# 32 of the 384 dense tokens take their down products from gathered rows; the gate product carries gate times activation; ScalarE builds three of eight one-hots

## The reference, cut to what matters

```python
q = (tokens @ w_query).reshape(Ntok, 8, 2, 128)
s = einsum('nhpd,hpkd->nhpk', q, sub_keys)          # 128 scores per head and half
s_top, i_top = top_k(s, 16)
cand = s_top[:, :, 0, :, None] + s_top[:, :, 1, None, :]   # 256 candidates
best, pos = top_k(cand, 16)                          # 16 experts per head: 128 per token
gate = softmax(best)
a = gelu(einsum('nd,nhkd->nhk', xb, expert_down[idx]))
out = einsum('nhk,nhkd->nd', gate * a, expert_up[idx])
```

## Time and profile before

| | |
|---|---|
| median of 3 runs | 1718.04 us |
| the profiled execution | 1719.09 us, its span 1717.4 us |
| PE busy | 1666.0 us, 97% |
| PEld (weight loads) busy | 1494.0 us, 87% |
| DVE busy | 1136.0 us, 66% |
| ACT busy | 672.5 us, 39% |
| POOL busy | 835.2 us, 49% |
| DMA | 423.38 MB, mean 247 GB/s |
| granted clock | 0.996 |

### The profile page before, as it was taken

How to read it: one execution, slowest core, us unless ns; L and a number is a source line. 1 busy time by engine, 2 the same in 40 slices (tenths; PEclk the granted TensorE clock), 3 DMA queues, 4 the chain that set the end, 5 groups by cost and what they waited for, 6 DMA issues and landing times.

```text
span 1717.4 us, 26045 instructions
## 1 busy us (share of the span) xinstructions
PE 1666.0 (97%) x8905; PEld 1494.0 (87%) x8905; DVE 1136.0 (66%) x2253; ACT 672.5 (39%) x972; POOL 835.2 (49%) x483
## 2 busy tenths in 40 slices
PE   7999999999999999999999999998999999999998
PEld 5788787868999999999999999997887878878886
DVE  4154552031295999796898888205878777878787
ACT  5342433342334343434444444333333333333333
POOL 3462374312255878786576666554333333434230
PEclk9999999999999999999999999999999999999999
DMA  4222243213635988887899999749999999999993
GB/s 172 89 96 74 74 148 123 86 50 101 207 133 189 297 285 276 285 286 255 312 322 324 332 339 348 263 146 335 321 355 335 352 330 352 339 348 351 342 347 146
DMA packets 148395, 423.38 MB, mean 247 GB/s; under 512 B 14320, under 2 KB 67568, under 8 KB 147440
## 3 DMA queue, kind: packets, MB, share of 16 engines
q1 hardware_dynamic: 93472, 237.53, 41.2%
q0 software_dynamic: 36864, 134.23, 21.8%
q10 hardware_dynamic: 18000, 50.89, 7.5%
HBM read 373.32 MB, written 49.28 MB: 246 GB/s over the span
## 4 chain that ended last, share of the span: by engine, by line
PE 58%; issue 20%; DMA 9%; POOL 9%; DVE 2%; ACT 1%; SPq 0%; POOLq 0%; ACTq 0%; DVEq 0%
PE psum L1136 18%; PE psum L1137 18%; PE psum L1138 18%; POOL w_low L367 9%; DMA arena<-down_rows,kept 4%; DMA arena<-hid_dram 4%; PE psum L1403 3%; DMA arena<-up_in 1%; DVE arena L1028 1%; PE psum L1389 1%; DMA kept<-down_in 1%; ACT w_high L459 0%; DVE arena L926 0%; DVE arena L1022 0%; DVE wgt_low L1067 0%
## 5 line engine op out<-in xcount | busy, mean ns | idle before, releaser
L367 POOL TENSOR_TENSOR w_low<-kept,w_high 128x1024 fp32r<-128x1024 f32 x212 | 517.4, 2443 | 481.2 <-ACT w_high L459 480.1
L1136 PE MATMUL psum<-hT_high,w_high 128*128 128x384 f32 (+1 forms) x1408 | 492.2, 350 | 7.3 <-POOL w_low L367 4.1
L1138 PE MATMUL psum<-hT_high,w_low 128*128 128x384 f32 (+1 forms) x1408 | 485.3, 345 | 0.0
L1137 PE MATMUL psum<-hT_low,w_high 128*128 128x384 f32 (+1 forms) x1408 | 485.1, 345 | 0.0
L1136 PE MATMUL psum<-up_high,wgt_high 128*128 128x512 f32 x768 | 301.2, 392 | 10.4 <-DVE wgt_low L1067 10.4
L1137 PE MATMUL psum<-up_low,wgt_high 128*128 128x512 f32 x768 | 299.8, 390 | 0.0
L1138 PE MATMUL psum<-up_high,wgt_low 128*128 128x512 f32 x768 | 299.7, 390 | 0.0
L459 ACT ACTIVATE w_high<-kept 128x1024 fp32r<-128x1024 f32 x212 | 224.1, 1058 | 192.5 <-DMA kept<-front_w 71.7
L1136 PEld LDWEIGHTS psum<-hT_high,w_high 128*128 128x128 f32 x1408 | 264.8, 188 | 19.2 <-issue 4.5
L1138 PEld LDWEIGHTS psum<-hT_high,w_low 128*128 128x128 f32 x1408 | 264.6, 188 | 10.3
L1137 PEld LDWEIGHTS psum<-hT_low,w_high 128*128 128x128 f32 x1408 | 264.9, 188 | 9.8 <-issue 0.5
(11 more groups left out here) (197 smaller groups left out, 1982.6 us busy)
## 6 DMA issues: line engine op xcount, KB each, us to landing
kept<-down_in SPq DMA_DIRECT2D x128, 512.0 KB
arena<-up_in SPq DMA_DIRECT2D x128, 512.0 KB
kept<-front_w SPq DMA_DIRECT2D x100, 512.0 KB
gate_dram<-arena ACTq DMA_DIRECT2D x6, 4096.0 KB, 15.9
arena<-gate_dram SPq DMA_DIRECT2D x32, 768.0 KB, 8.8
hid_dram<-arena ACTq DMA_DIRECT2D x112, 192.0 KB
arena<-hid_dram SPq DMA_DIRECT2D x112, 192.0 KB
kept<-x_in ACTq DMA_DIRECT2D x4, 512.0 KB, 5.0
```

The source lines that it names most:

```text
L367: nc.gpsimd.tensor_tensor(w_low[:, s, :], ring[:, s, :], w_hi[:, s, :].bitcast(F32), ALU.subtract).then_inc(low_ready, 1)
L1136: nc.tensor.matmul(out, lhs[0], rhs[0], start=first, stop=False)
L1137: nc.tensor.matmul(out, lhs[0], rhs[1], start=False, stop=False)
L1138: return nc.tensor.matmul(out, lhs[1], rhs[0], start=False, stop=last)
```

## The change

The last 32 tokens of dense tile 2 (the *edge*) leave the down product: `first_product`, Gelu, hid and its store have 352 columns (DE). Their 128 dot products are taken from gathered rows. 32 tokens × 128 slots are laid out as 128 partitions × 32 slots, so 32 more gathers and dots (`row_stream` mixes them with the 128 sparse ones: ROWS is 160); `edge_h` holds h of the 32 tokens four times over. ACT moves the edge's indices, and later its Gelu values back, by four small DMAs each. The edge's gates are multiplied by these Gelu values before they are transposed (`hk_last`), and the hid columns of the edge are ones in the up product, set by DVE's memsets in the buffers that it reads. For that, tile 2 is chosen first and transposed last, at step 24. AHEAD becomes 68, the steps carry 10 gathers in 6, the last 12 blocks up to two each.

In steps 0 to 43 DVE writes five of the eight second one-hots; ACT writes three (`hot_tails`) as relu(gate − gate·|iota − index|). 

```diff
 TILES_LAST = (ST, 0, 1, 2)
-EXP_AT = (16, 36, 56)
-TURN_AT = (20, 40, 60)
+CHOSEN = (DT - 1, 0, 1)
+EXP_AT = (16, 40, 64)
+TURN_AT = (24, 48, 68)
...
 RING_A, RING_B, RING_C = 5, 4, 8
-DOTS_SCORES = ((2, 2, 2, 2),) * 3
-DOTS_CAND = (1, 1, 1, 1)
-DOTS_HOT = (6, 6, 6)
-DOTS_A = 54
-DOTS_STEP = (2, 1, 2, 1, 2, 1)
-DOTS_B = GROUPS * sum(DOTS_STEP)
+EDGE = 32
+PARTS = P // EDGE
+EDGE_SLOTS = SLOTS // PARTS
+DE = DN - EDGE
+E0 = P - EDGE
+ROWS = SLOTS + EDGE_SLOTS
+DOTS_SCORES = (3, 2, 2, 2)
+DOTS_CAND = (1, 1, 1, 2)
+DOTS_HOT = 6
+DOTS_CHOICES = 60
+DOTS_A = 65
+DOTS_STEP = (2, 1, 2, 1, 2, 2)
+FIRST_EDGE = 32
+TAIL = 3
+TAIL_STEPS = DE // TB
+EDGE_GELU, EDGE_GATE, EDGE_TURN = 16, 19, 24
...
+def row_stream():
+    stream, own, edge = [], 0, 0
+    for k in range(ROWS):
+        if edge < EDGE_SLOTS and k >= FIRST_EDGE and (k % 2 == 0 or k >= DOTS_A):
+            stream.append((True, edge))
+            edge += 1
+        else:
+            stream.append((False, own))
+            own += 1
+    return stream
+STREAM = row_stream()
+EDGE_DONE = max(k for k in range(ROWS) if STREAM[k][0]) + 1
...
                     pool.wait_ge(dot_done, k - ahead + 1)
-                nc.gpsimd.indirect_dma_start(ring[slot], None, down_rows,
-                                             bass.IndirectOffsetOnAxis(idx3[:, k:k + 1].bitcast(U32), 0))\
+                edge, j = STREAM[k]
+                if edge and j == 0:
+                    pool.wait_ge(edge_moved, 2 * 16 * PARTS)
+                nc.gpsimd.indirect_dma_start(ring[slot], None, down_rows, bass.IndirectOffsetOnAxis(
+                    (edge_idx if edge else idx3)[:, j:j + 1].bitcast(U32), 0))\
...
-            pool.wait_ge(hk_ready, DT)
-            pool.wait_ge(hk_tr, DT)
+            pool.wait_ge(hk_ready, DT - 1)
+            pool.wait_ge(hk_tr, DT - 1)
...
                 for _ in range(DOTS_STEP[i % PER_GROUP] if i < DURING else 2):
-                    if k < SLOTS:
+                    if k < ROWS:
...
+            act.wait_ge(ffnn.h, DT)
+            for q in range(PARTS):
+                act.dma_start(edge_h[q * EDGE:(q + 1) * EDGE], hn[E0:P, DT - 1, :].rearrange("p (k n) -> p k n", k=KC))\
+                    .then_inc(edge_moved, 16)
...
                               r * 32 + 16 * (s // 2), r * 4 + (s + 3))
+            def turned_out(t, turned):
+                rows = turned.rearrange("p (a b) -> p a b", a=3)
+                step.put(nc.scalar.activation(tail_neg[:, t * P // TB:(t + 1) * P // TB, :],
+                                              rows[:, 2, :].rearrange("p (g e) -> p g e", e=TB)[:, :, TB - TAIL:TB],
+                                              ACT.Copy, scale=-1.0))
+                step.end()
+                nc.scalar.activation(hkT[:, :, t * P:(t + 1) * P], rows, ACT.Copy).then_inc(hkT_out, 1)
...
                 early_tiles(EXP_AT[n], TURN_AT[n])
-                act.wait_ge(hk_tr, n + 1)
-                nc.scalar.activation(hkT[:, :, n * P:(n + 1) * P], psum[:, 0, 0:3 * P].rearrange("p (a b) -> p a b", a=3), ACT.Copy)\
-                    .then_inc(hkT_out, 1)
+                if n == 0:
+                    act.wait_ge(idx_ready, 2)
+                    for q in range(PARTS):
+                        act.dma_start(edge_idx[q * EDGE:(q + 1) * EDGE, :],
+                                      idx_last[E0:P, q * EDGE_SLOTS:(q + 1) * EDGE_SLOTS]).then_inc(edge_moved, 16)
+                else:
+                    act.wait_ge(hk_tr, n)
+                    turned_out(CHOSEN[n], psum[:, 0, 0:3 * P])
+            def hot_tails(n, s):
+                if n:
+                    act.wait_ge(hot_tail, n)
+                step.end()
+                for e in range(TAIL):
+                    t = n * TB + TB - TAIL + e
+                    step.put(nc.scalar.activation(tail_off[:, e, :], iota, ACT.Abs, scale=-1.0, bias=hkT[:, 1, t:t + 1]))
+                step.end()
+                for e in range(TAIL):
+                    j = TB - TAIL + e
+                    t = n * TB + j
+                    ins = nc.scalar.activation(hot[:, s, 1, j * P:(j + 1) * P], tail_off[:, e, :], ACT.Relu,
+                                               scale=tail_neg[:, n, e:e + 1], bias=hkT[:, 2, t:t + 1])
+                    if e < TAIL - 1:
+                        step.put(ins)
+                ins.then_inc(hot_tail, 1)
...
+            act.wait_ge(hkT_out, DT - 1)
+            for n in range(HOTS):
+                hot_tails(n, n)
...
                 c, k = n // (CH // TB), n % (CH // TB)
-                early_at(AHEAD + n)
+                if n == EDGE_GELU:
+                    act.wait_ge(dot_done, EDGE_DONE)
+                    step(nc.scalar.activation(edge_gel, edge_dot, ACT.Gelu))
+                    for q in range(PARTS):
+                        act.dma_start(edge_back[E0:P, q * EDGE_SLOTS:(q + 1) * EDGE_SLOTS],
+                                      edge_gel[q * EDGE:(q + 1) * EDGE, :]).then_inc(edge_moved, 16)
+                if n == EDGE_TURN:
+                    act.wait_ge(hk_tr, DT)
+                    turned_out(CHOSEN[0], psum[:, 0, 0:3 * P])
+                    act.wait_ge(hkT_out, DT)
+                if AHEAD + n < SPILL:
+                    early_at(AHEAD + n)
+                else:
+                    keep(AHEAD + n)
...
                     dve.wait_ge(landed[slot], 16 * (n + 1))
-                    nc.vector.tensor_tensor_reduce(ring[slot], ring[slot], h_row, 1.0, 0.0, ALU.mult, ALU.add,
-                                                   dot3[:, k:k + 1]).then_inc(dot_done, 1)
+                    edge, j = STREAM[k]
+                    if edge:
+                        row = ring[slot].rearrange("p (k n) -> p k n", k=KC)
+                        ins = nc.vector.tensor_tensor_reduce(row, row, edge_h, 1.0, 0.0, ALU.mult, ALU.add,
+                                                             edge_dot[:, j:j + 1])
+                    else:
+                        ins = nc.vector.tensor_tensor_reduce(ring[slot], ring[slot], h_row, 1.0, 0.0, ALU.mult, ALU.add,
+                                                             dot3[:, j:j + 1])
+                    ins.then_inc(dot_done, 1)
...
             step(nc.vector.tensor_tensor(h_row, hn[:, ST, :], ffn_row, ALU.mult))
+            dve.wait_ge(edge_moved, 16 * PARTS)
+            step(nc.vector.tensor_tensor(edge_h, edge_h, ffn_row.rearrange("p (k n) -> p k n", k=KC), ALU.mult))
...
             kd = 0
-            for n in range(DT):
-                kd = choose(score[:, n, :], dense_k, kd, DOTS_SCORES[n], DOTS_CAND, DOTS_HOT[n], n)
-                gates_of(dense_k, hk[:, 2, :], n + 2).then_inc(hk_ready, 1)
-            assert kd == DOTS_A
+            for n, t in enumerate(CHOSEN):
+                kd = choose(score[:, t, :], dense_k, kd, DOTS_SCORES, DOTS_CAND, DOTS_HOT, hk if n else hk_last, max(n - 1, 0))
+                if n:
+                    gates_of(dense_k, hk[:, 2, :], n + 2).then_inc(hk_ready, 1)
+                else:
+                    nc.vector.scalar_tensor_tensor(idx_last.bitcast(U32), hk_last[:, 0, :], float(NK), hk_last[:, 1, :],
+                                                   ALU.mult, ALU.add).then_inc(idx_ready, 1)
+                    step(gates_of(dense_k, hk_last[:, 2, :], n + 2))
+            assert kd == DOTS_CHOICES
+            kd = dots(kd, DOTS_A - DOTS_CHOICES)
...
                     ALU.is_equal)
-                for j in range(n * TB, (n + 1) * TB):
+                for j in range(n * TB, (n + 1) * TB - (TAIL if n < TAIL_STEPS else 0)):
...
                 if n == 0:
+                    dve.wait_ge(hkT_out, DT - 1)
+                if n == EDGE_GATE:
+                    dve.wait_ge(edge_moved, 3 * 16 * PARTS)
+                    nc.vector.tensor_tensor(hk_last[E0:P, 2, :], hk_last[E0:P, 2, :], edge_back[E0:P, :], ALU.mult)\
+                        .then_inc(hk_ready, 1)
+                if n == CHOSEN[0] * P // TB:
...
                 kd = dots(kd, DOTS_STEP[n % PER_GROUP])
-            kd = dots(kd, SLOTS - kd)
+            kd = dots(kd, ROWS - kd)
+            for s in range(2):
+                dve.wait_ge(stored[s], 16 * (DCH // 2))
+            for ones_of in hid_ones:
+                step(nc.vector.memset(ones_of[:, :, DE:DN], 1.0))
...
             pe.wait_ge(pk_out, 8)
-            for n in range(DT):
-                with pe.Fori(TURN_AT[n - 1] // 4 if n else 0, TURN_AT[n] // 4) as r:
-                    for s in range(4):
-                        first_product(r * 4 + s, s)
-                pe.wait_ge(hk_ready, n + 1)
-                if n:
-                    pe.wait_ge(hkT_out, n)
+            def turn_chosen(n, where):
+                pe.wait_ge(hk_ready, n)
                 for j in range(3):
-                    ins = nc.tensor.transpose(psum[:, 0, j * P:(j + 1) * P], hk[:, j, :], ident)
+                    ins = nc.tensor.transpose(psum[:, 0, j * P:(j + 1) * P], where[:, j, :], ident)
```

(23 more changed lines are left out.)

63 lines of the change are left out of this document (39 added, 24 removed).

## The result

Median 1724.17 us (1715.59 to 1734.19) for 1717.88 (1713.43 to 1722.77), 20 runs each: ratio 1.0039, 95% interval 1.0021 to 1.0057. The change makes the kernel 0.4% slower; 1687 was forecast. The profiled execution has a span of 1719.8 us for 1717.4.

The account below looks back on a forecast made before the run. TensorE sets the pace, with the DMA engines a near second bound. A, B, C and gap go from 634.8 to 605.2 us (−29.6), the up product −1.7: 1719.1 becomes 1687.8 profiled, 1687 median, range 1673 to 1706.

Parts of the forecast that it names:

- held share of 0.977: DMA share held over 100 us of the up product, taken as ceiling: eight gate-product steps last 47.0 us, 47.3 taken.
- B: Stage of 48 steps, each one down block and one gate product: 285.5 us for 294.3; 280.5 at the result's marks.
- share of 0.92: DMA engines' share in eight typical steps of B before the change, read as a second bound near TensorE's.
- rival 1: DMA does not bind: B 274, kernel 1670 us; chance 0.13.
- A: Down-product blocks before the gate product, while DVE chooses experts: 263.7 us for 250.7; 268.7 at the result's marks.
- cover: DVE's 13.6 us left at A's end before the change; the added dots were claimed to fit.
- C: Last 12 down blocks after the gate product, with the gap before the up product: 56 us for 89.8.
- sum of bytes (52.7): DMA time of stores, gathers, down and up blocks and gate load meeting in C: 51.5 us, 52.7 at 0.977.
- gate load: First load of gates for the up product, waiting for the last dot; expected to end C after TensorE's last down block.
- rival 4: The shorter product buys nothing, a floor near 173 ns: kernel 1711 us; chance 0.03.
- rival 3: ACT becomes the bound in B; with table loads B is 360 and the kernel 1762 us; chance 0.05.
- rival 2: DMA keeps its share of 0.92: eight steps of B last 49.9 us, kernel 1712; chance 0.14.

Follow-up runs that it names:

- e8: Kernel before the change, with its 4 MB gate stores issued as eight 512 KB pieces, one a step (two in later ones): 1708.60 us, ratio 0.9953.
- e1: Changed kernel with the 32 edge dots reading h from PSUM instead of SBUF (values not the reference's): 1714.77 us, ratio 0.9972.
- e3: Changed kernel without the 32 edge gathers and dots (zeros in their place): 1711.05 us, ratio 0.9958.
- e4: Changed kernel with the 32 edge gathers kept and their dots left out: 1713.13 us, ratio 0.9970.
- e7: Changed kernel with each 4 MB gate store issued as eight 512 KB pieces, one a step (two in later ones): 1696.81 us, ratio 0.9871.
- e11: e9 with twelve gathered rows moved from the last 12 blocks to before the first gate product: 1705.49 us, ratio 0.9916.
- e2: Changed kernel with DVE building all eight one-hots and ACT none: 1731.38 us, ratio 1.0075.
- e5: Changed kernel with the 32 edge dots kept, on stale rows, and their gathers left out: 1714.37 us, ratio 0.9992.
- e13: e7 with each store piece cut as 16 partitions with their whole 32 KB, for 128 partitions with 4 KB: 1755.65 us, ratio 1.0206.
- e9: e7 with all 32 edge dots taken before the first gate product, reading h from PSUM; nothing left out: 1693.37 us, ratio 0.9858.

## Why the prediction was wrong

It failed in three steps, in this order of size.

1. **"This removes the stalls of about 1 us: with the lead that three buffers allow, DVE rides out a burst of the gate store", and beside it "At the held share of 0.977 eight steps last 47.0".** B missed by 14.2. The stalls of 1 us in each eight steps before were the burst, not DVE's load: e8 removes them with no other change (idle 13.1 to 6.2). The share of 0.92 was a mean over a burst and a lull, and I read it as room. A step shorter by 0.32 and with a ninth more gathers met the same burst, and the stalls grew from 0.7 to 1.3 us each to 2.1 to 3.5, four of the five with a stretch at the lower clock behind. The ceiling was wrong on the other side too: 371 GB/s over 135 us for the 350 of the earlier trace rows, so that with the store spread B is 273.0, below the 280.5 forecast and at the 274 of rival 1, though with the DMA engines at 0.98 to 1.00. The 358 GB/s per core that the Trainium skill (DMA: Bandwidth & Descriptors, section Where 436 GB/s comes from) gives, weighed in the prediction, is passed here: the measurement decides.

2. **"6 more dots at 1.21 ... It fits."** A missed by 13.7, of which e1, e3 and e4 each give 10.6 to 12.4 back (270.0 to 271.8 for 282.4). The 1.21 is the row of a dot with one operand in PSUM; an edge dot has both in SBUF and took 2.10. With 14 of them before 800 us at 2372 ns that is 14 × 1.15 = 16 us more, where the cover was 13.6 less what I had spent of it. That "TensorE would wait for DVE us for us" was right; what I did not see is the path, through POOL's queue to w_low. The form of the operand in the earlier trace rows (arena,psum) told it.

3. **C at 56.** 6.5 missed. The sum of bytes (52.7) didn't bind, the order did: w_low stands behind gathers in POOL's queue, and these wait for dots. The last burst made the longest of these waits, but with the store spread C is still 61.1 (e7), and with the 12 rows taken out of it 50.4 (e11). The gate load, which I thought last, is not: DVE had its first product at 1174.10, TensorE's last block ended at 1177.2.

What held: the 160.0 ns (rival 4 is out); no table load in B (rival 3 is out), and the tails, 0.99 + 1.27 = 2.3 us a step for the 1.6 to 2.0 reckoned, without harm (e2 is slower without them). Behind the first eight steps B shows 48.8 us for eight on average, near the 49.9 of rival 2, though not by its mechanism. The up product gained 4.7 for 1.7, but kernels with the same up product lie 8.8 us apart, so this is neither for nor against the forecast. Too cheap was ACT's issue of small moves: the four that bring the edge's Gelu values back took 5.41 us at 921.63 where I had put 0, with 1.2 us of waiting for TensorE behind it.

```profile
919.20 0.99 ACT L755 ACTIVATE kept<-kept,arena 128x128 f32<-128x128 f32 x3 [0.47 <-ACT arena L802]
920.22 1.26 ACT L760 ACTIVATE arena<-kept,arena 128x128 f32<-128x128 f32 x3
...
921.63 5.41 ACTq L788 DMA_DIRECT2D arena<-arena  x4
```

Open: how much of B is scatter between profiles (in the changed kernel and e1, e3, e4 and e5, with one store and the same late steps, it goes from 291.3 to 298.8); why a 32 KB packet of e13's pieces lasts 2.26 us for 1.28; what lengthens A in e11 beside its late exponential; and whether a balance of rows between that of e9 and of e11 would use C's 12 us over its floor, which was not tried.

## What to carry to other kernels

When the bound engine gets shorter by x, list every wait it covered, by the longest single one and not by a mean share: a DMA share of 0.92 can hide a stretch in which one queue has 87% of the engines. Here a 4 MB store was best cut and spread over the steps in which nothing waits for it; look for the effect of such a store in the queues it starves and in what stands behind it in its own. Leaving rows out tests the bytes of a stage only if the rows left out lie in that stage. Price an instruction by a row with the same operands in the same memories, and say which other engine reads there meanwhile.
